# Low halves of standing weights written and read 48 bytes into their SBUF buffers

## The reference

```python
for layer in range(2):                        # first stack
    z = rmsnorm(x, norm_mix[layer]) @ w_in[layer]              # 1024 x 2964
    ...                                       # four mixers on slices of z
    x = x + concat([o_a, o_b, o_c, o_d]) @ w_out[layer]        # 1024 x 1024
    h = rmsnorm(x, norm_ffn[layer])
    x = x + (silu(h @ w_gate[layer]) * (h @ w_up[layer])) @ w_down[layer]   # 1024 x 2816, twice, and back
x = rmsnorm(x, norm_final)
for i in range(4):                            # second stack
    h = (retention, conformer, short_conv)[i % 3](rms_norm(x, norm_g[i, 0]))
    x = x + rms_norm(h, norm_g[i, 1])
    h = square(relu(rms_norm(x, norm_g[i, 2]) @ mlp_w1[i])) @ mlp_w2[i]     # 1024 x 4096 and back
    x = x + rms_norm(h, norm_g[i, 3])
```

## Time and profile before

| | |
|---|---|
| median of 3 runs | 1992.46 us (1992.11 to 1994.58) |
| the profiled execution | 1993.23 us |
| its span (first to last instruction) | 1991.4 us |
| granted TensorE clock, mean | 0.999 of full speed |
| PE busy | 1971.4 us, 99% of the span |
| PEld, DVE, ACT busy | 84%, 67%, 48% |

### The profile page before, as it was taken

The page is one execution under the profiler, slowest core; times in us unless marked ns, Lnnn a source line. Parts: engine busy times, 40 slices in busy tenths (PEclk is TensorE's granted clock), DMA queues, the critical chain, the costliest instruction groups (busy, mean ns, idle before and its releaser), DMA issues.

```text
span 1991.4 us, 26383 instructions
## 1 busy us (share of the span) xinstructions
PE 1971.4 (99%) x11046; PEld 1670.7 (84%) x11046; DVE 1342.5 (67%) x1496; ACT 965.2 (48%) x1148; POOL 46.3 (2%) x89
## 2 busy tenths in 40 slices
PE   8999999999999999999999999999999999999998
PEld 6889888888988887788888688888888888778887
DVE  5876666687566775676568865566865667667565
ACT  6655444755544543354445554454544444345443
POOL 0000000000000000000000000000000000000000
PEclk9999999999999999999999999999999999999999
DMA  7425654523665555545657355547565555455653
GB/s 243 141 83 173 198 188 164 171 96 123 220 198 186 189 170 190 169 148 192 207 193 210 124 198 187 189 152 230 193 202 187 173 193 188 157 173 172 197 189 106
DMA packets 239558, 351.68 MB, mean 177 GB/s; under 512 B 15952, under 2 KB 134096, under 8 KB 239440
## 3 DMA queue, kind: packets, MB, share of 16 engines
q1 hardware_dynamic: 238864, 349.27, 53.8%
q10 hardware_dynamic: 576, 0.73, 0.1%
HBM read 344.83 MB, written 1.05 MB: 174 GB/s over the span
## 4 chain that ended last, share of the span: by engine, by line
PE 95%; DVE 1%; ACT 1%; DMA 1%; issue 0%; SPq 0%; DVEq 0%; ACTq 0%
PE psD L2199 20%; PE psD L2212 15%; PE psD L2213 15%; PE psD L2217 13%; PE psD L2203 9%; PE psD L2181 3%; PE psD L2180 3%; PE psD L2185 3%; PE psD L2215 2%; PE psD L2531 1%; DMA raw<-in_w_in 1%; PE psD L2479 1%; PE psD L2603 1%; PE psD L2604 1%; PE psD L2844 1%; PE psD L2296 1%
## 5 line engine op out<-in xcount | busy, mean ns | idle before, releaser
L1211 DVE TENSOR_TENSOR wl<-raw,wh 128x2048 fp32r<-128x2048 f32 (+2 forms) x327 | 723.5, 2219 | 258.1 <-ACT wh L675 257.4
L675 ACT ACTIVATE wh<-raw 128x2048 fp32r<-128x2048 f32 (+2 forms) x327 | 605.2, 1854 | 306.3 <-PE psD L2215 243.0
L2199 PE MATMUL psD<-AHL,wh 128*128 128x512 f32 x1664 | 589.2, 398 | 0.0
L2203 PE MATMUL psD<-AHL,wl 128*128 128x256 f32 x1560 | 438.1, 281 | 0.0
L2199 PEld LDWEIGHTS psD<-AHL,wh 128*128 128x128 f32 x1664 | 312.7, 188 | 77.5
L2212 PE MATMUL psD<-wh,HH 128*128 128x512 f32 x864 | 339.5, 393 | 0.1
L2213 PE MATMUL psD<-wl,HH 128*128 128x512 f32 x864 | 336.5, 389 | 0.0
L2203 PEld LDWEIGHTS psD<-AHL,wl 128*128 128x128 f32 x1560 | 294.6, 189 | 1.2
L2217 PE MATMUL psD<-wh,HL 128*128 128x512 f32 x735 | 286.6, 390 | 0.0
L2212 PE MATMUL psD<-wh,AHL 128*128 128x512 f32 (+3 forms) x516 | 199.3, 386 | 2.5 <-DVE AHL L1247 1.7
L2213 PE MATMUL psD<-wl,AHL 128*128 128x512 f32 (+3 forms) x516 | 192.8, 374 | 0.0
(11 more groups left out here) (403 smaller groups left out, 2252.0 us busy)
## 6 DMA issues: line engine op xcount, KB each, us to landing
raw<-in_mlp_w SPq DMA_DIRECT2D x128, 1024.0 KB, 5.4
raw<-in_ret_w_in SPq DMA_DIRECT2D x48, 1024.0 KB, 5.1
raw<-in_w_gate SPq DMA_DIRECT2D x20, 1024.0 KB, 5.3
raw<-in_w_up SPq DMA_DIRECT2D x20, 1024.0 KB, 5.3
raw<-in_w_down SPq DMA_DIRECT2D x20, 1024.0 KB, 5.2
raw<-in_ret_w_out SPq DMA_DIRECT2D x16, 1024.0 KB, 5.1
raw<-in_w_in SPq DMA_DIRECT2D x15, 1024.0 KB, 5.3
raw<-in_cf_w_pw SPq DMA_DIRECT2D x12, 1024.0 KB, 6.4
```

The costliest lines, as they stand in the source:

```text
L675: e.activation(wh[q % NHL][:, 0:kt * n], raw[q % NRAW][:, 0:kt * n], ACT.Copy).then_inc(*up("act_wh", q))
L1211: e.tensor_tensor(wl[q % NHL][:, 0:kt * n], raw[q % NRAW][:, 0:kt * n], wh[q % NHL][:, 0:kt * n].bitcast(F32), ALU.subtract).then_inc(*up( ...
L2199: e.matmul(o, hi[:, k, fs], both[:, k, :, :], start=k == 0, stop=False, skip_group_check=True)
L2203: e.matmul(o[:, S:2 * S], lo[:, k, fs], AH[:, k, :], start=False, stop=k == 7, skip_group_check=True)
```

## The change

The three `wl` buffers become 16 words (64 bytes) longer. For chunks with kt = 8 the low half is written, and read by the matmuls of `cols_half`, from word 12 of the buffer on, 48 bytes in; for all other chunks it starts at word 0 as before. `low_flat` and `low_tiles` give the place, and all readers of `wl` use them. The high halves and the data are what they were. Since every buffer declared behind a `wl` buffer moves up, the second `wl` buffer starts 64 bytes later, the third 128, and all that follow (`AHL`, `HH` and `HL` among them) 192. The instructions of every engine, their order, their waits and their shapes are the same in both kernels.

```diff
--- before.py
+++ after.py
@@ -270,7 +270,7 @@
 
         raw = [sb(f"raw{i}", [P, CH]) for i in range(NRAW)]
         wh = [sb(f"wh{i}", [P, CH], FR) for i in range(NHL)]
-        wl = [sb(f"wl{i}", [P, CH], FR) for i in range(NHL)]
+        wl = [sb(f"wl{i}", [P, CH + 16], FR) for i in range(NHL)]
         X = sb("X", [P, 2, DM])
         AHL = sb("AHL", [P, 16, S], FR)
         AH, AL = AHL[:, 0:8, :], AHL[:, 8:16, :]
@@ -347,6 +347,14 @@
         def tiles(t, c):
             kt, n = size(c)
             return t[c % NHL][:, 0:kt * n].rearrange("p (k n) -> p k n", k=kt)
+
+        def low_flat(c):
+            kt, n = size(c)
+            a = 12 if kt == 8 else 0
+            return wl[c % NHL][:, a:a + kt * n]
+
+        def low_tiles(c):
+            return low_flat(c).rearrange("p (k n) -> p k n", k=size(c)[0])
 
         def four_taps(e, x, js, signal):
 
@@ -1208,7 +1216,7 @@
                     count[0] += 1
                     kt, n = size(q)
                     e.wait_ge(*at("act_wh", q))
-                    e.tensor_tensor(wl[q % NHL][:, 0:kt * n], raw[q % NRAW][:, 0:kt * n], wh[q % NHL][:, 0:kt * n].bitcast(F32), ALU.subtract).then_inc(*up("dve_wl", q))
+                    e.tensor_tensor(low_flat(q), raw[q % NRAW][:, 0:kt * n], wh[q % NHL][:, 0:kt * n].bitcast(F32), ALU.subtract).then_inc(*up("dve_wl", q))
 
             def first_low(h):
 
@@ -2169,7 +2177,7 @@
             def cols_chunk(c, pair, k0, between=None):
 
                 kt, n = size(c)
-                hi, lo = tiles(wh, c), tiles(wl, c)
+                hi, lo = tiles(wh, c), low_tiles(c)
                 e.wait_ge(*at("dve_wl", c))
                 for k in range(kt):
                     kk = k0 + k
@@ -2281,7 +2289,7 @@
             def rows_first(c, i):
 
 
-                hi, lo = tiles(wh, c + 1), tiles(wl, c + 1)
+                hi, lo = tiles(wh, c + 1), low_tiles(c + 1)
                 for t in range(2):
                     ts, o = slice(t * P, (t + 1) * P), psD[2][:, t, :]
                     if t == 0:
@@ -2382,7 +2390,7 @@
 
                 def z_first(o):
 
-                    hi, lo = tiles(wh, 0), tiles(wl, 0)
+                    hi, lo = tiles(wh, 0), low_tiles(0)
                     e.wait_ge(*at("act_wh", "first"))
                     e.wait_ge(*at("dve_norm", "al", 0, 0, 0))
                     for k in range(4):
@@ -2901,7 +2909,7 @@
 
                 def by_pairs(n, o, t, j, event):
 
-                    hi, lo, ts = tiles(wh, n), tiles(wl, n), slice(t * P, (t + 1) * P)
+                    hi, lo, ts = tiles(wh, n), low_tiles(n), slice(t * P, (t + 1) * P)
                     for p in range(2):
                         e.wait_ge(*at("act_cf", "ah", 2 * j + p, t))
                         for k in (2 * p, 2 * p + 1):
```

## The result

The changed kernel takes 1988.43 us (median of 11 runs, 1987.61 to 1989.50) where the kernel before took 1992.53 (median of 11, 1991.65 to 1994.58). The ratio is 0.998, 95% interval 0.9971 to 0.9989: 4.1 us faster, a real but small gain, where 11.1 us were forecast. It lies in the stated range and near the rival "partly better".

A forecast was written before the change was run, and what follows sets the result against it. TensorE's stream was taken to bound the kernel. 11.1 us won on the pairs, with all other terms 0, took the median from 1992.46 to 1981.4 us; the whole range was 1971 to 1997.

The forecast's parts named there:

- partly better: Rival for the pairs: the cycle of three goes on at a mean of 347 to 351 ns; 1987 us, chance 0.14.
- What bounds the kernel: TensorE's stream sets the time, busy 1971.4 of 1991.4 us; no semaphore wait matters, only the time of single matmuls.
- The 48 bytes: Standing low halves in the 1664 pairs: the offset takes a pair from 353.3 to 346.7 ns, 11.1 us won.
- the two settled streams: Row matmuls of 512 columns at 226.7 ns and matmuls of 256 columns at 120.0, giving 346.7 ns for a pair.
- the 396-column rows: Row matmuls whose tiles start 0 to 48 bytes past multiples of 64, taking 177 to 183 ns: evidence that offsets matter.
- Settling as the reason: Pairs: moving the low half's address alone lets them fall into step, repeating one value, 0.35 us, without a cycle of three.
- The ten unsettled row matmuls: Row matmuls right behind pairs: 63 ns at each of some 35 changes, 2.2 us in all; might shrink, counted 0.
- 64, 128 and 192 bytes for all buffers behind: Moves of the other buffers: taken as 0, with up to 24 us lost if all row streams lose their step.
- DVE and the supply: DVE writes 104 low halves at the new place, about 2290 ns each, and still feeds the faster pairs; price 0.
- The best bound: Pairs: every one as short as the first behind settled row matmuls, 0.34 us; 22.2 us won.
- No change: Rival for the pairs: the address has no part and they stay at 353.3 ns; 1992.5 us, chance 0.22.
- Slower: Rival: low-half loads disturb the pairs' 512-column matmuls, up to 11.1 us lost, 2003.6 us; includes row-stream tail; chance 0.17.

The follow-up runs named there:

- offset_only: Kernel before with kt = 8 low halves at word 12 and low buffers 1024 bytes longer, so other buffers keep their places modulo 1024; 1981.95 us, ratio 0.9951.
- offset_32b: As offset_only, but with the low halves of kt = 8 at word 8 (32 bytes) instead of 12; 1983.01 us, ratio 0.9955.
- long_only: The changed kernel's longer low buffers, but every low half at word 0; 1995.99 us, ratio to the kernel before 1.002.
- mod_256: As offset_only, but with low buffers 64 words (256 bytes) longer instead of 256 words; 1981.78 us, ratio 0.9945.
- pairs_64_240: As cols_64b, but with the pairs' high halves at word 16 and low halves at word 60; 1968.15 us, ratio 0.9878.
- cols_64b: As offset_only, but high and low buffers each 256 bytes longer and both halves of cols_chunk's chunks at word 16; 1977.73 us, ratio 0.9924.

## Why the prediction was right and wrong

**What bounds the kernel: right.** TensorE's stream was the time, and waits took no part, except for 1.2 us of one wait that differs from kernel to kernel without a pattern.

**The 48 bytes: right in sign and size.** Forecast 11.1 us for pairs at 346.7 ns. In the changed kernel the pairs gave 10.3 us, and alone, in `offset_only`, pairs at 346.8 ns and 10 us. Bounding the pair by the two settled streams was a good step. That the value came out to the decimal is in part luck: nothing in the reasoning tied 346.7 ns to 48 bytes, and other distances give 340.0. The evidence was weaker than its use: the 396-column rows had become dearer with offset, and they said nothing on how a pair of 512 and 256 columns would answer.

**Settling as the reason: right in one kernel, not needed in others.** In `offset_only` one value repeats, as drawn. In the changed kernel the pairs still wander, since the moves gave each low buffer a distance of its own: the median chunk takes 348.3 ns a pair in the first buffer, 346.7 in the second, 340.9 in the third. And `offset_32b` has the full gain with two values that alternate. The test that the prediction set for itself ("the idea of settling is wrong if the time falls while three values still alternate") thus goes partly against it: what the gain hangs on is the mean over the cycle.

**The ten unsettled row matmuls: taken at 0, and they did shrink.** The first ten row matmuls behind pairs take 232.0 ns on average in the 35 places of the kernel before and 227.7 in `offset_only`, 1.5 us in all, though no distance of theirs has changed. In the changed kernel, where the rows have lost their pace themselves, they take 230.4.

**"64, 128 and 192 bytes for all buffers behind": the step that failed.** It was taken at 0, with a bound of 0 to 24 us. It measured +11.4 us on the row streams and -5.5 us on `cols_chunk`, 5.9 of the 7.0 us by which the forecast was off, and alone (`long_only`) +4.1 us in all. Three faults lie in that step. The first reason for the zero, that the pattern is the same in all three buffers though they are 8192 bytes apart, said nothing: 8192 is a multiple of 256, and `mod_256` shows that places repeat after 256 bytes, so the long streams of before held no distance but 0. The second reason, that the offsets with an effect in the earlier trace rows are all below 64 bytes, came from counting them modulo 64: the tiles lie 1584 bytes apart, so modulo 256 they stand at 0, 48, 96 and 144, and two of the three that differ are above 64. And the lower bound of 0 left out a gain, though nothing excluded one. With a middle value of the stated bound the forecast would have been 1993 us, 5 us off to the other side instead of 7; the honest consequence was a forecast with less weight on one value. The edit with the biggest reach was treated as a side effect of the edit with a name.

**DVE and the supply: right.** 2290 ns as before, no new pattern of waits.

**The best bound was real.** The 340 ns of the first pair behind a settled row stream was taken as an end that need not be reached. `pairs_64_240` holds it over 96 pairs.

**The rivals.** "No change" fell with `offset_only`. The Trainium skill (SBUF — State Buffer, section "SBUF: two separate sides") has TensorE read its moving and its stationary operand through independent ports that wait on no one. What the prediction drew from it, that nothing should change, isn't what was measured: distances between the two operands move this kernel from 2008.9 to 1966.6 us with the same instructions. Whether a port waits, or something behind the ports, no run shows. The same page's 16-byte lines (Trainium skill, section "Specifications (TRN2)") can't explain it either, since all offsets tried are whole lines. "Slower" named the wrong place: the loss was not in the pairs but in the rows, for which it kept 0.03. "Partly better" gave 1987 us, nearest to the 1988.4 measured, but by another way: full gain at the pairs, given back elsewhere.

## What to carry to other kernels

Where matmuls follow each other without gaps, compare the distance from start to start with columns divided by the clock rate: a steady surcharge, or a cycle of values, is a cost that no wait shows. Then look at the addresses that are read together, the moving operand and the weight tile loaded beside it, modulo 256 bytes, and try a few distances for each kind of stream by itself. Try them in the whole kernel, since a stream's pace depends on the one before it too. And cost every byte by which an edit moves other buffers: here padding by 256 or 1024 bytes left all other streams as they were, and padding by 64 was a second change that nobody meant to make.

## What the runs showed of the hardware that was not expected

- The pace of a gapless float32r matmul stream depends on the distance between its moving operand and the standing tile that is loaded meanwhile: pairs from 340.0 to 353.3 ns, 512-column rows from 226.7 to about 235, 256-column matmuls from 113 to 120, at the same granted clock (1.00).
- Of the addresses it is this distance that counts: a common shift of 160 bytes changed nothing, shifts by 256 and 1024 bytes changed nothing, 32, 48 and 64 bytes each changed the pairs by 6 ns.
- It isn't the distance alone. At distances 192 and 192 the median chunk of `cols_chunk` takes 341.0 ns for three matmuls in one buffer of the changed kernel and 353.4 in `cols_64b`; and rows at distance 0 take 232.0 or 227.7 ns behind pairs, by how the pairs ran.
- The same distance suits one stream and spoils another: 192 bytes of move make `cols_chunk` 4 ns faster a matmul and the rows 3 ns slower.
- Most settled streams come out at multiples of 6.67 ns, which are 16 columns at 2.4 GHz: matmuls or pairs of 120.0, 226.7, 340.0 and 346.7 ns are 18, 34, 51 and 52 times that, and the cycle of before with its mean of 353.3 is 53. The changed kernel's rows, 0.70 us for three, are no such multiple at the finer reading (15 in 3.49 us, so 698 ns for three, 104.7 times). No run here says why.
